# Scores of two attentions from rounded parts stacked over the full contraction height

## The reference

```python
# first block: 16 heads of width 64, dilated windows (three of them, merged by their softmax denominators)
q = rope_partial(heads(aq, 16), pos) * (64 ** -0.5)
k = rope_partial(heads(ak, 16), pos)
res = [dilated_band_attention(q, k, v, w, d) for (w, d) in ((128, 1), (512, 4), (2048, 16))]
#   in each: s = q @ k^T; s = where(valid, s, -1e30); softmax; o = p @ v; lse
o_att = sum over the three of softmax(lse) * o;   y_att = o_att * silu(ag)

# each of the two later layers: 4 heads with two query/key pairs of width 64 each, causal
s = einsum('bqhcd,bkhcd->bhcqk', q, k); s = where(kpos <= qpos, s, -inf)
p = softmax(s); w = p[:, :, 0] - lam * p[:, :, 1]; o = w @ v
```

## Time and profile before

| | |
|---|---|
| median of 3 runs | 3124.75 us (3123.7 to 3125.0) |
| span of the profiled execution | 3121.8 us, 3 us under that median |
| PE busy | 97% of the span |
| DVE, ACT, POOL busy | 53%, 39%, 42% |
| DMA | 99 GB/s mean |
| mean granted TensorE clock | 0.992 |

### The profile page before, as it was taken

How to read it: one execution, slowest core, us unless ns; L and a number is a source line. 1 busy time by engine, 2 the same in 40 slices (tenths; PEclk the granted TensorE clock), 3 DMA queues, 4 the chain that set the end, 5 groups by cost and what they waited for, 6 DMA issues and landing times.

```text
span 3121.8 us, 44761 instructions
## 1 busy us (share of the span) xinstructions
PE 3041.7 (97%) x15518; PEld 2410.3 (77%) x15518; DVE 1641.8 (53%) x2261; ACT 1227.8 (39%) x2164; POOL 1316.8 (42%) x1006
## 2 busy tenths in 40 slices
PE   8999999999999999999999999999999999999997
PEld 6877778777777787777777777788777777777886
DVE  5377666554554414657565664461275646645412
ACT  6445444333334333444233333453332333334532
POOL 4444344333334244452434344444534434443444
PEclk9999999999999999999999999999999999999998
DMA  6222212222222323233322222233342222222322
GB/s 240 103 84 98 81 69 82 79 73 76 74 74 81 122 94 135 95 109 121 128 71 97 76 81 84 79 114 129 108 160 90 85 88 81 85 81 81 145 98 94
DMA packets 60872, 307.70 MB, mean 99 GB/s; under 512 B 5712, under 2 KB 6096, under 8 KB 29520
## 3 DMA queue, kind: packets, MB, share of 16 engines
q1 hardware_dynamic: 38224, 259.54, 23.2%
q10 hardware_dynamic: 22528, 46.60, 4.3%
HBM read 287.77 MB, written 18.35 MB: 98 GB/s over the span
## 4 chain that ended last, share of the span: by engine, by line
PE 48%; issue 27%; POOL 14%; DVE 7%; DVEq 2%; ACT 1%; POOLq 0%; DMA 0%; ACTq 0%; SPq 0%
PE z L302 37%; POOL w_low L239 13%; DVE work L1428 2%; DVEq L1510 1%; DVE work L1417 1%; PE z L318 1%; PE turned L302 1%; PE scores L526 1%; PE scores L499 1%; PE o_bank L506 1%; DVE work L1579 1%; PE scores L302 1%; PE scores L536 1%; PE o_bank L546 1%; PE v_bank L335 1%
## 5 line engine op out<-in xcount | busy, mean ns | idle before, releaser
L239 POOL TENSOR_TENSOR w_low<-w_raw,w_high 128x512 fp32r<-128x512 f32 x932 | 1256.0, 1352 | 1785.0 <-ACT w_high L688 1778.3
L302 PE MATMUL z<-u_high,w_high 128*128 128x512 f32 x3408 | 1371.7, 402 | 2.9 <-POOL w_low L239 2.2
L302 PE MATMUL z<-u_high,w_low 128*128 128x512 f32 x3408 | 1329.0, 390 | 0.0
L302 PE MATMUL z<-u_low,w_high 128*128 128x512 f32 x3408 | 1327.7, 390 | 0.0
L688 ACT ACTIVATE w_high<-w_raw 128x512 fp32r<-128x512 f32 x928 | 578.5, 629 | 1275.1 <-PE z L302 1177.4
L302 PEld LDWEIGHTS z<-u_high,w_high 128*128 128x128 f32 x3408 | 640.1, 188 | 149.2 <-issue 16.9
L302 PEld LDWEIGHTS z<-u_low,w_high 128*128 128x128 f32 x3408 | 640.3, 188 | 143.7 <-issue 14.4
L302 PEld LDWEIGHTS z<-u_high,w_low 128*128 128x128 f32 x3408 | 639.6, 188 | 136.1
L1579 DVE TENSOR_TENSOR work<-work 128x512 f32<-128x512 f32 x87 | 99.7, 1146 | 363.8 <-ACT work L935 350.6
L1241 DVE TENSOR_TENSOR work<-z,work 128x512 f32<-128x512 f32 x110 | 76.1, 692 | 166.1 <-PE z L302 145.1
L1269 DVE SCALAR_TENSOR_TENSOR work<-z,work 128x512 f32<-128x512 f32 x56 | 38.7, 692 | 188.9 <-PE z L302 188.3
(11 more groups left out here) (265 smaller groups left out, 3106.9 us busy)
## 6 DMA issues: line engine op xcount, KB each, us to landing
w_raw<-in_wt SPq DMA_DIRECT2D x241, 1024.0 KB, 4.8
out_hT<-work ACTq DMA_DIRECT2D x8, 1024.0 KB, 7.6
work<-out_hT ACTq DMA_DIRECT2D x8, 1024.0 KB, 10.3
work<-in_xT SPq DMA_DIRECT2D x4, 1024.0 KB, 17.9
e_scratch<-work ACTq DMA_DIRECT2D x1, 4096.0 KB, 19.5
work<-in_xT ACTq DMA_DIRECT2D x4, 1024.0 KB, 10.5
work<-in_gw ACTq DMA_DIRECT2D x2, 1792.0 KB, 10.0
work<-in_dec ACTq DMA_DIRECT2D x12, 256.0 KB, 2.6
```

Of the source, the lines that this page charges most:

```text
L239: pool.tensor_tensor(WL[:, 4 * q:4 * q + 4, :], RAW[:, t.odd, 512 * q:512 * q + 512].rearrange("p (k c) -> p k c", k=4), WH[:, 4 * q:4 * q ...
L302: mm = pe.matmul(bank[:], w[:, k, :], u[:, k, :], start=(k == 0 and n == 0), stop=(k == KT - 1 and n == 2))
```

## The change

The float32 scores become sums of float32r products, as in the projections. For head A (partitions 0 to 63 of `QN` and `KN`) row `QT` gets the query's high part in partitions 0 to 63 and its low part in 64 to 127. One key row holds the key's high part in both halves, another the key's low part in both halves. Two accumulating matmuls over 128 partitions then give (high + low) x high + (high + low) x low. Head B has the same with the halves exchanged, in `KTR`. This takes four rows of `work` for the keys (rows 7 to 10 for att, 9 to 12 for dif).

`take_heads` goes for att and dif and stays for ret. In its place, at p=13, ACT makes six copies of 64 partitions to float32r (`high_heads`), and DVE six subtractions of 64 partitions (`low_heads`), which wait for ACT's copies by pairs and signal `qt_ready` or `dqt_ready` at the end.

```diff
 def att_scores(j, a):                                            # PE
-    o = 64 * hd
-    pe.matmul(SC[hd][:], row(QT)[o:o + 64, a * P:(a + 1) * P], row(KTR)[o:o + 64, :],
-              start=True, stop=True).then_inc(sem("s_done"), 1)
+    for n in range(2):
+        mm = pe.matmul(SC[hd][:], WR[:, QS[hd], a * P:(a + 1) * P], WR[:, KP["qt_ready"] + 2 * hd + n, :],
+                       start=(n == 0), stop=(n == 1))
+    mm.then_inc(sem("s_done"), 1)
...
+def high_heads(take, j, made, high_done, scored):                # ACT, p=13, behind its work of that place
+    act.wait_ge(sem(made), j * 2 + 2)
+    if not isinstance(j, int) or j:
+        act.wait_ge(sem(scored), j * 8)
+    kp = KP[take]
+    copy(WR[LOW, QS[0], :], row(QN)[LOW])
+    copy(WR[UP, QS[1], :], row(QN)[UP], high_done)
+    copy(WR[LOW, kp, :], row(KN)[LOW])
+    copy(WR[UP, kp + 2, :], row(KN)[UP], high_done)
+    copy(WR[UP, kp, :], row(KN)[LOW])
+    copy(WR[LOW, kp + 2, :], row(KN)[UP], high_done)
...
+def low_heads(take, j, made, high_done):                         # DVE, p=13, in place of take_heads
+    def low_half(r, to, source, high, at):
+        return v.tensor_tensor(WR[to, r, :], row(source)[at], WR[at, high, :].bitcast(F32), ALU.subtract)
+    kp = KP[take]
+    v.wait_ge(sem(high_done), j * 3 + 1)
+    low_half(QS[0], UP, QN, QS[0], LOW)
+    low_half(QS[1], LOW, QN, QS[1], UP)
+    v.wait_ge(sem(high_done), j * 3 + 2)
+    low_half(kp + 1, LOW, KN, kp, LOW)
+    low_half(kp + 1, UP, KN, kp, LOW)
+    low_half(kp + 3, UP, KN, kp + 2, UP)
+    v.wait_ge(sem(high_done), j * 3 + 3)
+    low_half(kp + 3, LOW, KN, kp + 2, UP).then_inc(sem(take), 1)
```

More of the change, by code:

```diff
@@ L865, in _, with step @@
             WORK = {"hg": hg_work, "att": att_work, "ret": ret_work, "dif": dif_work}
-            def step(t, gate=None, gates=None, hg=None, work=None, j=None, apart=False, between={}, **kw):
+            def step(t, gate=None, gates=None, hg=None, work=None, j=None, apart=False, heads=None, between={}, **kw):
                 for p in range(16):
@@ L879, in step @@
                         WORK[work](j, p, **kw)
+                    if heads is not None and p == 13:
+                        high_heads(*heads)
                     if hg is not None and p in (3, 7, 11):
@@ L1046, in _ @@
                 step(Tile(T_HG, (4, i)), hg=i, work="hg", j=i - 1)
-            step(Tile(T_ATT), gate=8, work="hg", j=HG_HEADS - 1)
-            step(Tile(T_ATT + 4), gate=9, work="att", j=0)
+            step(Tile(T_ATT), gate=8, work="hg", j=HG_HEADS - 1, heads=att_heads(0))
+            step(Tile(T_ATT + 4), gate=9, work="att", j=0, heads=att_heads(1))
             with act.Fori(2, PAIRS - 1) as i:
-                step(Tile(T_ATT, (4, i)), gate=i + 8, work="att", j=i - 1, late=i - 2)
+                step(Tile(T_ATT, (4, i)), gate=i + 8, work="att", j=i - 1, late=i - 2, heads=att_heads(i))
             def operand_quarter(q):
@@ L1068, in next_output @@
                 high(Tile(T_OUT + 1), q, 4 * T_OUT + 2 * q + 2)
-            step(Tile(T_OUT - 4), gate=PAIRS + 7, work="att", j=PAIRS - 2, late=PAIRS - 3, apart=True,
+            step(Tile(T_OUT - 4), gate=PAIRS + 7, work="att", j=PAIRS - 2, late=PAIRS - 3, apart=True, heads=att_heads(PAIRS - 1),
                  between={p: lambda q=q: operand_quarter(q) for p, q in ((13, 0), (14, 1), (15, 2))})
@@ L1261, in gate_tile, with rotated @@
                 v.drain()
-            def rotated(t, dst, cos, sin, half, scale):
+            def rotated(t, dst, cos, sin, half, scale, made=None):
                 z = Z[t.odd]
@@ L1489, in _, with att_heads, dif_heads, step @@
             WORK = {"hg": hg_work, "att": att_work, "ret": ret_work, "dif": dif_work}
-            def step(t, rot=None, scales=None, gate=None, hg=None, work=None, j=None, lru=None, take=None, fin=None, open_gate=False, between={}, **kw):
+            def att_heads(j):
+                return "qt_ready", j, "qk_made", "qk_high"
+            def dif_heads(j):
+                return "dqt_ready", j, "dqk_made", "dqk_high"
+            def step(t, rot=None, scales=None, gate=None, hg=None, work=None, j=None, lru=None, take=None, heads=None, fin=None,
+                     open_gate=False, between={}, **kw):
                 for p in range(16):
@@ L1525, in step @@
                         take_heads(take)
+                    if heads is not None and p == 13:
+                        low_heads(*heads)
                     if fin is not None and p == 1:
@@ L1752, in _ @@
             sc1 = (ATT_HD ** -0.5, 1.0)
-            step(Tile(T_ATT), rot=tb, scales=sc1, take="qt_ready", gate=(8, 8), work="hg", j=HG_HEADS - 1)
+            step(Tile(T_ATT), rot=tb, scales=sc1, heads=att_heads(0), gate=(8, 8), work="hg", j=HG_HEADS - 1)
             def low_some(p):
@@ L1757, in low_some @@
                     low_tile(m, 16, MIX[:], None)
[L1759 removed]
+            step(Tile(T_ATT + 4), rot=tb, scales=sc1, heads=att_heads(1), gate=(9, 9), work="att", j=0)
             with v.Fori(2, PAIRS - 1) as i:
[L1761 to L1762 removed]
+                step(Tile(T_ATT, (4, i)), rot=tb, scales=sc1, heads=att_heads(i), gate=(i + 8, i + 8), work="att", j=i - 1, late=i - 2)
+            step(Tile(T_OUT - 4), rot=tb, scales=sc1, heads=att_heads(PAIRS - 1), gate=(15, 15), open_gate=True, work="att", j=PAIRS - 2,
                  late=PAIRS - 3)
```

38 lines of the change are left out of this document (24 added, 14 removed).

## The result

The changed kernel takes 3142.3 us (median of 4 runs, 3140.9 to 3144.8); the kernel before, run beside it, 3124.25 us (3123.7 to 3125.0). The ratio is 1.006, with a 95% interval of 1.0047 to 1.0073: slower by 18 us. The profiled execution has a span of 3141.7 us against 3121.8. The forecast was 3137.8 us, slower, with a range of 3120 to 3152.

What follows compares the result with a forecast made beforehand. PE, busy for 97% of the span, was taken as the bound. -14.5 + 12.6 + 4.6 + 2.9 + 6.9 + 0.5 = +13.0 us: span 3121.8 to 3134.8, plus 3 us between span and median gives 3137.8 us; range 3120 to 3152.

Steps and rivals of the forecast that it cites:

- PE's scores: Score blocks in att and dif: four full-height float32r records each save PE 14.5 us (5.8 to 15.9).
- ret-to-dif, 2: Two ret-to-dif steps: PE's value turning waits for queued copies and subtractions, 6.3 us later each, 12.6 in all.
- the clock there: Behind the two ret-to-dif waits: granted clock 0.50 for 4.6 us of work, 2.3 us lost each, 4.6 (0 to 6.8).
- T_OUT - 4: At that step six subtractions replace two copies: PE waits 2.9 us more (1.9 without POOL, 4.1 with two operations).
- ordinary dif, 6: Six ordinary dif steps: PE waits 0.6 or 1.7 us by POOL hits; middle 1.15, 6.9 in all (0 to 10).
- ordinary att, 6: Six ordinary att steps: subtractions end at 728.4, needed at 728.39; 0.1 us each, 0.5 in all (0 to 7).
- the two other choices in the prediction: Dif score records: every narrow one costs 0.226 us (saving 1.3 us), or 128 columns cost 0.067 (saving 11.4).
- Faster: Rival, chance 0.10: copies and subtractions of 64 partitions cost half, no clock loss; -8.8 us, 3116.
- Even: Rival, chance 0.20: waits take their lower bounds, no clock loss, ordinary steps nothing; -2.2 us, 3122.5.
- Costlier: Rival, chance 0.13: narrow float32r records cost as much as wide, POOL hits DVE twice in dif steps; +29 us, 3154.

Runs made afterwards that it cites:

- filled: The changed kernel with 28 more TensorE passes behind the first quarter of each first differential step, where TensorE idles for the heads; 3138.11 us, ratio 1.0047.
- pe_alone: The changed kernel without low parts: full-height score passes on rounded queries and keys, the six copies and six subtractions gone; 3110.56 us, ratio 0.9959.
- same_half: The changed kernel with the same copies and subtractions reordered, so that more neighbours write and read the same half of the partitions; 3150.14 us, ratio 1.009.
- act_early: The changed kernel with ScalarE's six copies in the last retention step at quarter 12 in place of 13; 3138.87 us, ratio 1.0051.
- six_moved: The changed kernel, heads at quarter 10 of the last retention step and 12 of T_OUT-4, that retention step's logarithm and exponential at 15; 3138.4 us, ratio 1.0046.

## Why the prediction was right

Each term by its place in the sum, forecast against measured. The measured ones are waits and starts of PE in the traces.

| term | forecast | measured | by |
|---|---|---|---|
| PE's scores | -14.5 | -13.8 | span with the passes alone |
| ret-to-dif, 2 | +12.6 | +13.6 | 7.08 + 7.50, less 0.68 and 0.31 |
| the clock there | +4.6 | +5.0 | starts in `filled`; 4 by medians |
| T_OUT - 4 | +2.9 | +3.5 | 3.69 less 0.17 |
| ordinary dif, 6 | +6.9 | +7.5 | 2.21 + 0.91 + 4 x 0.86, plus 6 x 0.16 |
| ordinary att, 6 | +0.5 | +3.2 | waits of 0.36 to 0.42, plus 6 x 0.16 |
| the clock at T_OUT - 4 | - | +0.8 | start of the next stage against `pe_alone` |
| the clock behind the dif wait of 2.21 | - | +1.7 | starts against `pe_alone`, before and behind the stretch at 0.50 |

Forecast in sum: +13.0; measured +21.5, and the span grew by 19.9. The terms come from different kernels and overlap, which makes about these 1.6 us: `pe_alone` itself waits 0.54 us at T_OUT - 4, where the kernel before waits 0.17, so 0.4 is counted twice; the starts of the changed kernel against `pe_alone` give 2.4 and 1.7 us for the clock behind the two long waits, 0.9 less than `filled` does; and the changed kernel is 0.4 us ahead of `pe_alone` before the first score, for no cause that was looked for. The 0.16 is the overlap of the turning with the record ahead of it (0.39 us long, the next one 0.23 behind it), which a wait also takes away; the forecast counted waits alone.

*The scores.* The step was right, with its choice of 0.12 us for a 256-column record and 0.17 for 384. For 128 columns it took 0.11; the trace has 0.11 inside a head and 0.14 from the first head to the second, so the block takes 0.48 us for 0.44, as long as one of 256 keys. The nearest row decided well: the two other choices in the prediction, 0.226 and 0.067, are excluded.

*Ret-to-dif.* The chain is the forecast one, link by link. Mis-sized was the pitch: six copies 3.83 us and not 3.22, six subtractions with one POOL hit 5.16 and not 4.8. The prediction took it from full-height neighbours, and `same_half` shows why that was wrong. For T_OUT - 4 the prediction gives 2.9 us without a row for where the subtractions begin; it measured 3.5.

*The clock.* It was carried over from the earlier trace rows as half of 4.6 us. `filled` gives 5.0 by starts, and 3.5 to 4.2 by medians, the first with each kernel against the kernel before beside it. The clock was not carried to the two shorter waits, of 3.69 us at T_OUT - 4, where it cost some 0.8, and of 2.21 us in the first dif step, where it cost 1.7. Behind the second it doesn't always fall: five kernels have this wait, and in `act_early` and `six_moved` the stretch behind it is at 1.00.

*Ordinary steps.* In dif the sum was right partly by luck, by the middle of a range that took one or two POOL hits as equally likely. The trace has one hit in five steps and two hits in the first alone; what made the five dearer than the 0.6 reckoned for one hit is the pitch again. In att the forecast of 0.1 us a step was the weakest: an end at 728.4 against a need at 728.39 had no slack for 0.10 us more on each of six subtractions, so six waits of 0.36 came. This term is the largest miss, 2.7 us of the 6.9 by which the span was too low (3134.8 for 3141.7). The time was too low by 4.5 only, since between span and median lay 3 us before and 0.6 after.

*The bounds.* "Faster" asked for operations that cost half on 64 partitions: 0.63 and 0.69 us each, it is excluded. "Even" asked for no clock loss and no POOL hits: `filled` and the 5.16 exclude both. "Costlier" asked for narrow records as dear as wide ones: excluded by the 0.48 us of a 256-key block.

No errors cancelled in the sum: every wait was taken a little too short, the gain a little too large, and 2.5 us of clock were left out, nearly as much as att's 2.7. Only the distance from span to median worked the other way, by 2.4 us, and that was luck.

What the prediction did not say is how far the loss could be mended. The four-subtraction kernels show that: 12 us hang on two subtractions, 7 on the place of the copies, and the last 10 down to `pe_alone`'s 3110.6 were not reached by any order tried. As these traces read, DVE's queue between the recurrence and the gate bank has no room for the 2.8 us of four subtractions; no run shows that no other order would do. Whether another engine making some of the parts would reach it was not tried.

## What to carry to other kernels

Price a saving on the busiest engine against the operations that feed it, at the steps where that engine already waits for the feeder: there every added microsecond is paid in full, and the clock can be paid on top (here behind the waits of 2.21 us and more, though not in every kernel). What counts is the time from the last input to the last operation behind it, so count what is queued there and give it the shortest tail; then look whether a step moved away from one wait only pushes the next one in the same queue, and whether it makes a third engine start sooner, on top of the operations that are late. Where two causes hide behind each other (copies and subtractions here), undo both before judging either.

## What the hardware showed unexpectedly

- Consecutive operations on 64 partitions started sooner only where both write the same half and read the same half: 0.52 to 0.54 us from copy to copy on ACT and 0.61 on DVE (`same_half`), otherwise 0.62 to 0.66 and 0.70. Full-height ones have 0.52 and 0.60.
- A DVE subtraction that begins while POOL subtracts lasts 1.0 us longer: of the six in a row, without a hit 5 x 0.70 + 0.69 = 4.19 us, one is hit in every step of the changed kernel (5.16 to 5.19) but the first dif one (two, 6.16). One that is already under way when POOL begins is not longer: the fifth in the att steps has POOL beside its last 0.22 us and lasts 0.69.
- In `filled`, 28 passes whose result nobody reads kept the granted clock at 1.00, where it had been 0.50 for 10.2 us, and won 4 us over two such places.
